# Prompt attention of a hybrid decoder layer: values stationary in column halves, probabilities scaled before their transposes

## What is computed

```python
def block(args):                      # one block of 128 queries, all heads
    idx, ql, qp = args
    sc = _scores(ql, qp, c_kv, k_pe)  # float32, times SOFTMAX_SCALE
    q_pos = idx * Q_BLOCK + jnp.arange(Q_BLOCK)
    sc = jnp.where(k_pos[None, :] <= q_pos[:, None], sc, -jnp.inf)
    pr = jax.nn.softmax(sc, axis=-1).astype(c_kv.dtype)
    return jnp.einsum("bhqk,bkr->bqhr", pr, c_kv)
...
o_a = jnp.einsum("bshr,rhv->bshv", o_lat, lw["w_uv"]).reshape(b, s, MLA_HEADS * V_DIM) @ lw["w_oa"]
```

## Time and profile before

| | us |
|---|---|
| median of 3 runs (lowest 4290.12, highest 4294.96) | 4291.56 |
| the profiled execution's span, first to last instruction | 4288.3 |
| this phase in it, from its first mask row to the next phase's first issue | 186.4 |

### The profile page before, as it was taken

One profiled execution on the slowest core, in us unless ns is written; L12 is line 12 of the kernel. 1 busy time (PEld: TensorE's weight loads), 2 busy tenths in 40 slices (PEclk: granted clock), 3 DMA queues, 4 the chain that ended last, 5 costly groups with the idle time before them and its releaser, 6 DMA issues. The chain is left out here.

```text
span 4288.3 us, 63446 instructions
## 1 busy us (share of the span) xinstructions
PE 3703.7 (86%) x24803; PEld 3412.1 (80%) x24803; DVE 2050.5 (48%) x3135; ACT 1014.0 (24%) x1555; POOL 638.0 (15%) x543
## 2 busy tenths in 40 slices
PE   7999999789997997999567686867896999999967
PEld 7999999789994576888466665656895999999957
DVE  3434343532224344888475757574515443434453
ACT  3111111120001354666311111111413111111131
POOL 0000000200000005777121313131001000000112
PEclk9999999899998898999788788878897999999978
DMA  2111111222222005655201010100412111111032
GB/s 92 50 40 50 40 50 40 80 90 96 89 90 79 8 11 160 186 179 177 72 3 25 8 25 8 25 8 9 170 35 111 45 50 40 50 40 50 30 118 94
DMA packets 148414, 281.27 MB, mean 66 GB/s; under 512 B 58164, under 2 KB 97140, under 8 KB 147092
## 3 DMA queue, kind: packets, MB, share of 16 engines
q1 hardware_dynamic: 126324, 237.26, 16.6%
q0 software_dynamic: 12288, 37.77, 3.0%
q10 hardware_dynamic: 9536, 2.44, 0.3%
HBM read 233.48 MB, written 43.80 MB: 65 GB/s over the span
## 5 line engine op out<-in xcount | busy, mean ns | idle before, releaser
L79 PE MATMUL f_psg<-f_u_hi,f_w_hi 128*128 128x352 f32 x1056 | 347.4, 329 | 62.5 <-DVE f_w_lo L336 60.9
L428 DVE TENSOR_TENSOR c_x<-c_x,f_psd 128x352 f32<-128x352 f32 x480 | 246.2, 519 | 319.2 <-PE f_psd L81 319.2
L79 PE MATMUL f_psd<-f_hid_hi,f_w_hi 128*128 128x352 f32 x1056 | 350.9, 332 | 18.2 <-DVE c_x L428 9.8
L332 ACT ACTIVATE f_w_hi<-f_raw 128x1024 fp32r<-128x1024 f32 x132 | 136.6, 1054 | 915.6 <-PE f_psd L81 352.1
L79 PE MATMUL f_psu<-f_u_hi,f_w_hi 128*128 128x352 f32 x1056 | 343.1, 325 | 5.4 <-DVE f_w_lo L336 5.4
L80 PE MATMUL f_psg<-f_u_lo,f_w_hi 128*128 128x352 f32 x1056 | 342.8, 325 | 0.0
L81 PE MATMUL f_psg<-f_u_hi,f_w_lo 128*128 128x352 f32 x1056 | 342.5, 324 | 0.0
L80 PE MATMUL f_psd<-f_hid_lo,f_w_hi 128*128 128x352 f32 x1056 | 342.2, 324 | 0.0
L81 PE MATMUL f_psd<-f_hid_hi,f_w_lo 128*128 128x352 f32 x1056 | 341.7, 324 | 0.0
L80 PE MATMUL f_psu<-f_u_lo,f_w_hi 128*128 128x352 f32 x1056 | 340.6, 323 | 0.0
L81 PE MATMUL f_psu<-f_u_hi,f_w_lo 128*128 128x352 f32 x1056 | 340.3, 322 | 0.0
(11 more groups left out here) (402 smaller groups left out, 8488.7 us busy)
## 6 DMA issues: line engine op xcount, KB each, us to landing
f_raw<-in_ffn_gu SPq DMA_DIRECT2D x88, 512.0 KB, 4.1
sa_pages<-in_cache SPq DMA_DIRECT2D x256, 144.0 KB
f_raw<-in_ffn_d SPq DMA_DIRECT2D x44, 512.0 KB, 3.9
proj<-in_out SPq DMA_DIRECT2D x36, 528.0 KB, 2.9
inw_raw<-in_w_in_units SPq DMA_DIRECT2D x36, 512.0 KB, 4.0
h<-c_x SPq DMA_DIRECT2D x24, 528.0 KB, 2.7
r_old<-h SPq DMA_DIRECT2D x3, 4224.0 KB, 12.9
c_x<-proj SPq DMA_DIRECT2D x16, 528.0 KB
```

What stands on the lines that cost most here:

```text
L79: pe.matmul(out, w_hi, x_hi, start=start, stop=False)
L332: act.activation(w_hi[:, u % 3, :], raw[:, u % 3, :], ACT.Copy).then_inc(hi_done, 1)
L428: dve.tensor_tensor(a, a, ps_d[:, n % 2, 0:TB], ALU.add).then_inc(added, 1)
```

## The change

Three things are altered, all within the phase. First, `normalise` is now done for each item, and on the probabilities: VectorE takes the reciprocal of the item's sum and multiplies `pa_prob` by it in place, and `values(n)` waits for `scaled` in place of `exped`. Second, `weighted` works on a pair of heads every second item: a tile of `v` with 64 columns is the weight, the transposed probabilities (128 columns) stream, and the two heads go to the lower and the upper 64 partitions of `pa_o`, by turns. `pa_prob_t` has four buffers and `pa_o` two. Third, `pa_o` then already has the layout that is stored, so `turn_out`, its PSUM tile and `pa_o_tok` go, and ScalarE copies `pa_o` to `pa_o_t`.

```diff
             def values(n):
...
                     if g == 0:
-                        pe.wait_ge(exped, n + 1)
+                        pe.wait_ge(scaled, n + 1)
...
             def weighted(n):
                 qb, h = items[n]
                 if h == 0:
-                    wait(pe, o_out, qb)
-                pe.wait_ge(t_out, last_group[n] + 1)
+                    wait(pe, o_out, qb - 1)
+                pe.wait_ge(t_out, last_group[n + 1] + 1)
+                c = slice((h // 2) * P, (h // 2 + 1) * P)
                 for k in range(qb + 1):
-                    mm = pe.matmul(ps_o[:, h * V_DIM:(h + 1) * V_DIM], prob_t[:, n % 2, k * P:(k + 1) * P],
-                                   v[:, k, h * V_DIM:(h + 1) * V_DIM], start=(k == 0), stop=(k == qb))
-                mm.then_inc(pv_done, 1)
-
-            def turn_out(qb):
-                pe.wait_ge(o_out, qb + 1)
-                wait(pe, ot_out, qb)
-                for c in range(4):
-                    mm = pe.transpose(ps_ot[:, c * P:(c + 1) * P], o_tok[:, qb % 2, c * P:(c + 1) * P],
-                                      env.ident[:, :])
-                mm.then_inc(ot_done, 1)
+                    for i in range(2):
+                        r = slice(i * V_DIM, (i + 1) * V_DIM)
+                        mm = pe.matmul(ps_o[r, qb % 2, c], v[:, k, (h + i) * V_DIM:(h + i + 1) * V_DIM],
+                                       prob_t[:, (n + i) % 4, k * P:(k + 1) * P], start=(k == 0), stop=(k == qb))
+                mm.then_inc(pair_done, 1)
...
                 values(n)
-                if n > 0:
-                    weighted(n - 1)
-                    if items[n - 1][1] == 2 and items[n - 1][0] > 0:
-                        turn_out(items[n - 1][0] - 1)
-            weighted(len(items) - 1)
-            turn_out(NB - 1)
+                if n > 0 and n % 2 == 0:
+                    weighted(n - 2)
+            weighted(len(items) - 2)
...
+            def normalise(n):
+                qb, h = items[n]
+                k = n % 2
+                dve.wait_ge(exped, n + 1)
+                dve.reciprocal(rinv[:, k:k + 1], rsum[:, k:k + 1]).then_inc(inv_done, 1)
+                dve.wait_ge(inv_done, n + 1)
+                dve.tensor_scalar(prob[:, k, 0:(qb + 1) * P], prob[:, k, 0:(qb + 1) * P], rinv[:, k:k + 1], None,
+                                  ALU.mult).then_inc(scaled, 1)
 
             dve.wait_ge(mask_in, 16)
             softmax_max(0)
-            for n, (qb, h) in enumerate(items):
+            for n in range(len(items)):
                 if n + 1 < len(items):
                     softmax_max(n + 1)
-                if h == 0 and qb > 0:
-                    normalise(qb - 1)
-            normalise(NB - 1)
+                normalise(n)
```

More of the change, by code:

```diff
@@ L1210, in prompt_attention_phase @@
         prob = sb("prob", [P, 2, SEQ])
[L1211 to L1214, removed]
+        prob_t = sb("prob_t", [P, 4, SEQ])
+        rmax, nmax, rsum = sb("rmax", [P, 2]), sb("nmax", [P, 2]), sb("rsum", [P, 2])
+        rinv = sb("rinv", [P, 2])
+        o_t = sb("o_t", [P, 2, 4, P])
         ps_s = ctx.enter_context(nc.psum_tensor("pa_s", [P, 2, SEQ], F32))
         ps_t = ctx.enter_context(nc.psum_tensor("pa_t", [P, 2, 512], F32))
-        ps_o = ctx.enter_context(nc.psum_tensor("pa_o", [P, 512], F32))
-        ps_ot = ctx.enter_context(nc.psum_tensor("pa_ot", [P, 512], F32))
+        ps_o = ctx.enter_context(nc.psum_tensor("pa_o", [P, 2, 512], F32))
         mask_in = sem("mask_in")
@@ L1221, in prompt_attention_phase @@
         exped, t_done, t_out = sem("exped"), sem("t_done"), sem("t_out")
-        pv_done, inv_done, o_out, ot_done, ot_out = (sem(n) for n in
-            ("pv_done", "inv_done", "o_out", "ot_done", "ot_out"))
+        inv_done, scaled, pair_done, o_out = sem("inv_done"), sem("scaled"), sem("pair_done"), sem("o_out")
         stored = [sem("stored0"), sem("stored1")]
@@ L1236, in _ @@
             for qb in range(NB):
-                sp.wait_ge(ot_out, qb + 1)
+                sp.wait_ge(o_out, qb + 1)
                 sp.dma_start(oa_dram[:, :, qb * P:(qb + 1) * P], o_t[:, qb % 2, :, :]).then_inc(stored[qb % 2], 16)
@@ L1339, in exponent @@
                     act.wait_ge(t_done, last_group[n - 2] + 1)
+                    act.wait_ge(inv_done, n - 1)
                 act.activation(prob[:, k, 0:(qb + 1) * P], ps_s[:, k, 0:(qb + 1) * P], ACT.Exp,
                                bias=nmax[:, k:k + 1], scale=SOFTMAX_SCALE,
-                               accum_out=rsum[:, qb, h:h + 1]).then_inc(exped, 1)
+                               accum_out=rsum[:, k:k + 1]).then_inc(exped, 1)
             def copy_out(qb):
-                act.wait_ge(ot_done, qb + 1)
+                act.wait_ge(pair_done, (qb + 1) * (H // 2))
                 wait(act, stored[qb % 2], 16 * (qb // 2))
-                act.activation(o_t[:, qb % 2, :, :], ps_ot[:, :].rearrange("p (c t) -> p c t", c=4),
-                               ACT.Copy).then_inc(ot_out, 1)
+                act.activation(o_t[:, qb % 2, :, :], ps_o[:, qb % 2, :].rearrange("p (c t) -> p c t", c=4),
+                               ACT.Copy).then_inc(o_out, 1)
             exponent(0)
@@ L1356, in _ @@
                     act.wait_ge(t_done, m + 1)
-                    wait(act, pv_done, n - 1)
-                    act.activation(prob_t[:, n % 2, g * 512:g * 512 + w * P], ps_t[:, m % 2, 0:w * P],
+                    wait(act, pair_done, n // 2 - 1)
+                    act.activation(prob_t[:, n % 4, g * 512:g * 512 + w * P], ps_t[:, m % 2, 0:w * P],
                                    ACT.Copy).then_inc(t_out, 1)
-                if h == 4 and qb > 0:
+                if h == 2 and qb > 0:
                     copy_out(qb - 1)
```

## The result

| | us |
|---|---|
| the changed kernel, median of 4 runs (4459.44 to 4466.66) | 4463.52 |
| the kernel before on the same chip, median of 4 runs (4290.12 to 4294.96) | 4292.17 |
| ratio, with its 95% interval | 1.0393 (1.0378 to 1.0408) |
| the phase, from its first mask row to the next phase's first issue, now 1447.37 to 1808.35 | 361.0 |

The change makes the kernel 171 us slower. The forecast was 4460 with a range of 4393 to 4512. The phase grew from 186.4 to 361.0 us, 174.6 of the 176.5 us between the two spans, so the rest of the program is as it was.

The account below looks back on a forecast made before the run. TensorE was taken to bound the phase, VectorE and ScalarE being hidden. To 4291.6 us the prediction added 96 for the loop of TensorE and VectorE and 73 for the lower clock: 4460 us, range 4393 to 4512.

Parts of the forecast that it names:

- The loop: In each item TensorE and VectorE take turns, as transposes now wait for the scaling: +96 us net at the full clock.
- the list: The times from scores through mask, bias, scaling, transposes and half a pair, summing to 4.03 (block 3) and 6.51 us (block 7).
- the turns around the pairs: TensorE's changes of tiling mode around each pair of weighted sums, allowed 0.1 us a pair.
- The clock: TensorE's idle waits in the phase lower its granted clock: +73 us, 21 in blocks 0 to 2 and 52 in 3 to 7.
- the rival of the full clock alone: The phase runs at the full clock from block 2 on, as before: about 4398 us, chance 0.15.
- the line 1.55 + 0.62k + 0.436k: Time of an item with k key tiles: 1.55 + 0.62k us at full clock, 0.436k more at the lower clock.
- The half: Blocks 3 to 7 were given half of the full lower-clock loss, 52 us.
- The saving on TensorE: Weighted sums on two overlapping column halves save 31 us, dropped output transposes 3.5: TensorE some 35 us shorter.
- The end: From the last mask row to the next phase: 12.6 us against 14.0, a small gain.
- no overlap of the halves: The sums keep their old price, 31 us more: 4419 us at full clock or about 4500, chance 0.06.
- Turns of a whole matmul's 0.27 us in and out: Each tiling turn around a pair costs 0.27 us: 64 turns 17 us in place of 3, forecast 14 us higher.
- The faster rival: TensorE stays the bound, the scaling lying beside its work: about 4254 us, chance 0.03.

Follow-up runs that it names:

- e4: The changed kernel with 1 to 3 idle matmuls of 512 columns on TensorE ahead of its wait for the scaling: 4391.6 us.
- e2: The changed kernel with reciprocal and scaling of item n moved ahead of the mask, maximum and bias of item n+1 on VectorE: 4313.7 us.
- e3: The changed kernel with TensorE putting out the scores two items ahead, before the transposes of item n: 4275.5 us.
- e6: The kernel of e4 with a second scaling, by 1.0 in place, behind the first in every item: 4426.8 us.
- e5: The kernel of e4 with all key tiles of the lower half issued before all of the upper half, not by turns: 4412.0 us.
- e1: The changed kernel without reciprocals and scaling, probabilities left unnormalised, the transposes waiting for the exponentials again: 4284.5 us.
- e7: The kernel of e3 with each pair of sums cut in two, half the key tiles behind each item's transposes: 4272.3 us.
- e9: The kernel of e7 with one idle matmul of 256 columns ahead of each item's transposes in blocks 0 and 1: 4267.3 us.

## Why the prediction was right, point by point

**The loop (first term, +96 us).** Right: e4 has it alone, 97.5 us. The mechanism is shown by three edits that leave the work as it is or add to it: another place on VectorE takes 150 us off (e2), another place on TensorE 188 (e3), a second scaling adds its full length (e6). Its terms, from the item shown above, against those of the list: scores to mask 2.02 us for 1.98; mask to bias 1.59 for 1.59; bias to scaling 0.26 for 0.30, as the reciprocal of one column takes 0.153 us and not 0.19; the scaling 0.753 and 0.487 us for 0.75 and 0.48; from its end to the transposes 0.06 for 0.10; transposes 0.93 for 0.87. A step without a pair is 1777.14 - 1771.63 = 5.51 us where the sum without the pair gives 5.59; in blocks 1 and 3 of e4 it is 2.37 for 2.52 and 3.42 for 3.54. That is some 8 us too much over 64 items, and it happens to cancel the 8 us by which the turns around the pairs were undersized, as told below. To meet 97.5 us so closely is in part luck.

**The clock (second term, +73 us).** Right in sum, 72 us, and near in its parts. One reading was off: I let the lower clock last through block 1 of the kernel before, but the earlier trace rows end at 1469.10, and from there to the end of the block at 1473.95 the clock was 1.00; that touches the rival of the full clock alone. For blocks 1 and 2, wholly at the lower clock, the line 1.55 + 0.62k + 0.436k gives 3.66 and 4.72 us an item; the trace has 3.68 and 4.72. For blocks 3 to 7 I had taken half of the 104.6 us. The items took 5.21, 6.36, 6.94, 7.34 and 7.52 us against 4.03, 4.65, 5.27, 5.89 and 6.51 on the line, which is 7.02 us, times eight 56 us, a little over half. With the 20 us of blocks 0 to 2 (I had 21) that is the 76.5 us between the profiled phases. But it was not spread evenly: some three quarters of the possible loss in block 4, under a third in block 7. The half was a choice between two ends, and a third or two thirds would have been as well founded, 17 us less or more; that the median came within 2 us is in part luck. The clock of 0.6 to 0.9 in these blocks was what the profile then showed.

**The saving on TensorE.** The pace of the halves was right: at the end of the phase 32 instructions take 1.97 us, of which the last one's way through the array is 0.27, so they start 0.055 us apart. The reading of the earlier trace rows was loose, though. The prediction said that the delta rule puts them out by turns; its lines 2459 to 2461 give six instructions to one half and then six to the other, and the trace shows them interleaved, which fits the short distance that e5 measured. For the changed kernel, which does go by turns, it made no difference. The turns between the pair and what stands around it were undersized: in e4 a step with a pair is 0.78, 1.00, 1.21 and 2.09 us longer than one without, for k = 2, 3, 4 and 8, which is 0.34 + 0.218k. The 0.218k are the sums at 0.0545 us each; the 0.34 us are the turns, where I had allowed 0.1, and 32 pairs make that 8 us. In the changed kernel the saving shows only as a shorter TensorE part of each turn. As a gain over the kernel before it was too large: I gave TensorE as the bound 4254, and e1 and e3, which come near that case, gave 4284 and 4275. What was missing is that a pair every second item leaves TensorE short of work in the items between, and the 8 us of the turns.

**The end.** Wrong in sign: 1808.35 - 1793.30 = 15.05 us, where I had 12.6 and it had been 14.0. The rows show the larger part of it: the second to last pair took 3.07 us, partly at the lower clock, where the last one took 1.97, and I had reckoned the end at the full clock. The rest stays open. The term is 2.4 us off in 171.

**The rivals.** The full clock at 4398 and no overlap of the halves are ruled out by the windows and by e5. Turns of a whole matmul's 0.27 us in and out would be 0.54 us a pair; e4 has 0.34 with everything that a pair adds beside its pace, between my 0.1 and that bound. The Trainium skill, page "TensorEngine Tiling (Array Packing)", section Key Properties, says that a change of tiling mode drains TensorE. The 0.34 us agree with that, and are the most that it can cost here. The faster rival named its point of decision as the scaling ahead of the mask. e2 did exactly that and gave 4314, not 4254, because VectorE then waits for its own item's exponentials. The point that decides is another: that the scores are two items ahead (e3).

## What to carry to other kernels

When a step is put between two engines that were a step apart, write down the order of both and see whether each now waits for what the other does last; if so the costs add up, whatever their busy shares, and see whether looking one item further ahead on one engine opens the loop: here that took back all of the 171 us and some 18 more. An alternation also costs TensorE's clock, which here was a second loss of three quarters of the first. To tell the two apart, put idle matmuls into the wait.

## What the runs showed of the hardware

- Matmuls of 64 weight columns and 128 float32 columns ran at 0.055 to 0.060 us each when lower and upper half went by turns, and at 0.101 us when fourteen for one half stood ahead of fourteen for the other. In the delta rule the halves also ran at 0.055 us with six instructions in a row for each. By e5 about four on either side of a joint overlap, which with joints at both ends covers a run of six. Matmuls for different halves thus pass side by side over a short distance only; I had expected either all or nothing.
- Idle matmuls that fit into a wait made a kernel 72 us faster (e4). The clock rose within block 0 of e4, whose mean was 0.82, and stayed at 1.00 although TensorE was busy in only 16.86 of 21.90 us of block 1.
- A pair of sums on column halves between full-width matmuls cost 0.34 us beside its pace of 0.0545 us an instruction, the same for 8 instructions and for 32 (e4).
- The same block with the same work, cut into other pieces, had a mean clock of 0.97 in one kernel (e3, block 2) and of 0.75 in another (e7), in one profiled execution of each. Part of the gain of evening out TensorE's work went with it, until idle work brought the clock to 1.00 (e9).
- Scaling float32 from SBUF to SBUF on VectorE took 0.287 us for 128 elements and 0.753 for 1024 with a factor per partition, and 0.228 and 0.694 with a constant factor (e6).
